# A hybrid decoder on one core: a second set of slots for the experts' down weights, an unrolled pair of rounds, and norms by token halves

## The reference

```python
def swiglu(h, w_gate, w_up, w_down):
    return (jax.nn.silu(h @ w_gate) * (h @ w_up)) @ w_down

def moe_swiglu(h, router_w, w_gate, w_up, w_down):
    ...
    for e in range(N_EXPERTS):
        y = swiglu(tokens, w_gate[e], w_up[e], w_down[e])
        out = out + combine[:, e:e + 1].astype(tokens.dtype) * y
```

## Time and profile before

| | us |
|---|---|
| median of 3 runs (2118.75 to 2121.64) | 2120.52 |
| the profiled execution, its own time | 2123.79 |
| its span | 2122.0 |
| TensorE matmuls busy | 1998.0 (94%) |
| TensorE weight loads busy | 1767.4 (83%) |
| VectorE / ScalarE / GpSimd busy | 403.7 / 271.6 / 87.8 |

### The profile page before, as it was taken

The page is one execution under the profiler, slowest core; times in us unless marked ns, Lnnn a source line. Parts: engine busy times, 40 slices in busy tenths (PEclk is TensorE's granted clock), DMA queues, the critical chain, the costliest instruction groups (busy, mean ns, idle before and its releaser), DMA issues.

```text
span 2122.0 us, 66421 instructions
## 1 busy us (share of the span) xinstructions
PE 1998.0 (94%) x31038; PEld 1767.4 (83%) x31038; DVE 403.7 (19%) x896; ACT 271.6 (13%) x572; POOL 87.8 (4%) x174
## 2 busy tenths in 40 slices
PE   7999989998999899999899969999999999999997
PEld 6888867887777688888678869998989898989896
DVE  3235331111000142353311130101010100000001
ACT  1213213001000112132220010000000000000001
POOL 4010111000000001011000000000000000000000
PEclk9899999999999999999899989999999999999999
DMA  7313112436741332221134549999999999999996
GB/s 232 119 42 120 41 41 67 132 119 223 234 157 40 119 107 74 80 80 42 41 111 147 216 169 397 407 407 407 407 407 407 407 407 407 407 407 407 407 407 251
DMA packets 214758, 482.90 MB, mean 228 GB/s; under 512 B 11582, under 2 KB 110092, under 8 KB 214668
## 3 DMA queue, kind: packets, MB, share of 16 engines
q1 hardware_dynamic: 214668, 481.54, 60.9%
HBM read 480.46 MB, written 1.05 MB: 227 GB/s over the span
## 4 chain that ended last, share of the span: by engine, by line
PE 83%; DMA 6%; DVE 4%; SPq 4%; ACT 1%; issue 1%; POOL 0%; DVEq 0%
PE bank L1089 29%; PE bank L598 21%; PE bank L1058 7%; DMA pool<-in_moe_w_down_dram 6%; PE bank L660 5%; PE bank L1012 4%; PE bank L1040 4%; SPq L1996 3%; PE bank L1027 3%; PE bank L1198 1%; PE bank L623 1%; SPq L2001 1%; PE bank L652 1%; PE bank L976 0%; DVE pool L1713 0%
## 5 line engine op out<-in xcount | busy, mean ns | idle before, releaser
L1089 PE MATMUL bank<-pool 128*64 128x80 f32 x21504 | 757.1, 234 | 32.8 <-DMA pool<-in_moe_w_down_dram 26.4
L1089 PEld LDWEIGHTS bank<-pool 128*64 128x64 f32 x21504 | 752.4, 138 | 38.8 <-issue 28.8
L598 PE MATMUL bank<-hnT,pool 128*128 128x256 f32 x1984 | 464.1, 389 | 1.6 <-DVE hnT L1537 1.6
L598 PEld LDWEIGHTS bank<-hnT,pool 128*128 128x128 f32 x1984 | 376.9, 194 | 62.6 <-issue 8.1
L1058 PEld LDWEIGHTS bank<-hnT,pool 128*128 128x128 f32 x704 | 133.7, 190 | 27.8 <-issue 9.6
L1058 PE MATMUL bank<-hnT,pool 128*128 128x256 f32 x704 | 155.5, 379 | 0.8 <-DVE hnT L1537 0.8
L1907 DVE TENSOR_TENSOR pool<-pool,bank 128x320 f32<-128x320 f32 x32 | 15.6, 488 | 639.1 <-ACT pool L1492 639.1
L660 PEld LDWEIGHTS bank<-pool 64*64 64x64 f32 x3008 | 96.0, 135 | 18.1 <-issue 11.5
L660 PE MATMUL bank<-pool 64*64 64x64 f32 (+1 forms) x3008 | 105.2, 221 | 5.6 <-DVE pool L1563 4.6
L1492 ACT ACTIVATE pool<-bank 128x320 f32<-128x320 f32 x32 | 14.0, 437 | 677.2 <-PE bank L1089 677.2
L547 POOL TENSOR_TENSOR pool<-pool,level_mask 128x256 f32<-128x256 f32 x72 | 52.0, 735 | 838.8 <-DVE pool L1639 538.4
(11 more groups left out here) (324 smaller groups left out, 1284.0 us busy)
## 6 DMA issues: line engine op xcount, KB each, us to landing
pool<-in_moe_w_up_dram SPq DMA_DIRECT2D x128, 896.0 KB, 16.6
pool<-in_moe_w_gate_dram SPq DMA_DIRECT2D x128, 896.0 KB, 16.5
pool<-in_w_in_dram SPq DMA_DIRECT2D x66, 1024.0 KB, 5.4
pool<-in_moe_w_down_dram SPq DMA_DIRECT2D x64, 1024.0 KB, 16.7
pool<-in_moe_w_down_dram SPq DMA_DIRECT2D x32, 1536.0 KB, 18.6
pool<-in_ffn_w_gate_dram SPq DMA_DIRECT2D x11, 1024.0 KB, 11.3
pool<-in_ffn_w_up_dram SPq DMA_DIRECT2D x11, 1024.0 KB, 7.8
pool<-in_ffn_w_down_dram SPq DMA_DIRECT2D x11, 1024.0 KB, 9.7
```

The lines of the kernel that those rows point to most:

```text
L598: ins = mm(ps[:, s * T:(s + 1) * T], w[:, k, (j + s) * P:(j + s + 1) * P], hnT[:, k, :], start=(k == 0), stop=(k == KD - 1))
L1089: ins = mm(bank[rows, cs], w[:, rows], rhs, start=start, stop=stop, skip_group_check=True)
```

## The change

- **Down weights in two sets.** `down_slot(n, p)` has a set for even and one for odd rounds. The second set's first load (round 1 of the first pass) is asked for after the last output projection; in the loop the down weights of round r + 2 are asked for when round r is done with its set. The places are where the merge's tensors lay.
- **PE's loops.** The loop over rounds runs NR // 2 = 2 times over a body of two rounds (p = 0 and 1). The loop over passes runs one time less, and the last pass is a second copy of the body, without the next pass's gather and selection rows. DVE's program is split the same way. SP's loop over rounds is written out.
- **Norms by token halves.** The output projection runs token tile by token tile; squares, Ln, Exp, scaling and transposes are issued per tile, those of tile 0 before the last quarter of the projection; the table load comes first. So too behind the dense part, where a signal is given after tile 0's last down matmuls.
- **RWKV order.** Its tiles are projected in the order (6, 2, 3, 0, 1, 4, 5). The LoRA matmuls come after 2 steps instead of all 26 that are left, then 8 own steps, kk2, the other 16, and 4 attention steps in place of 5 + 2 + 6; each of the two solver runs takes 3 instead of 2.
- **End.** x times the gain goes to its own place (xf) beside the squares; the factor is then applied to tile 0 by ACT and to tile 1 by DVE.

```diff
-        def down_slot(n):
-            lo = 2 * KH * HSLOT
+        def down_slot(n, p):
+            lo = 2 * KH * HSLOT + p * FB * D
             return pool[:, lo + 2 * n * D:lo + min(2 * n + (3 if n == 2 else 2), FB) * D].rearrange("p (f n) -> p f n", n=D)
...
-                all_of(projections)
-                some(steps, 5)
+                some(projections, 2)
                 lora_in.wait(pe, l, 1)
                 oa_ready.wait(pe, l, 2)
                 if l == 0:
...
-                some(steps, 2)
+                some(projections, 8)
                 kk2_ready.wait(pe, l, 1)
                 for q in range(2):
                     kk2_mm.by(mm(B[4 + q][:, :], same_chunk[:], rsq[:, 2 * q:2 * q + 2, :], start=True, stop=True))
-                some(steps, 6)
+                all_of(projections)
+                some(steps, 4)
...
-                    solver(l, 1 + q, steps, (2, 4))
+                    solver(l, 1 + q, steps, (2, 3, 4))
...
-                for half in range(2):
-                    for t in range(NT):
-                        if half == 0 and t == 0:
-                            merge_step.wait(pe, l, 12)
-                            oc_ready.wait(pe, l, 4)
-                        bank = B[2 * half + t]
+                merge_step.wait(pe, l, 12)
+                oc_ready.wait(pe, l, 4)
+                for t in range(NT):
+                    for half in range(2):
+                        bank = B[2 * t + half]
                         for s in range(2):
                             n = L[l]["out"][2 * half + s]
-                            arrived(n)
+                            if t == 0:
+                                arrived(n)
                             for k in range(KD):
                                 ins = mm(bank[:, s * SW:(s + 1) * SW], mT[:, k, t * P:(t + 1) * P], weights(n)[:, k, :],
                                          start=(k == 0), stop=(k == KD - 1))
                         xo_mm.by(ins)
-                    for s in range(2):
-                        release(L[l]["out"][2 * half + s], xo_mm)
+                        if t == 1:
+                            for s in range(2):
+                                release(L[l]["out"][2 * half + s], xo_mm)
+                        if t == 1 and half == 0:
+                            transposes_of_hn(l, 1, 0)
+                xo_ready.wait(pe, l, 2)
+                transposes_of_hn(l, 1, 1)
...
+                        if t == 0 and f == FFD // P - 1:
+                            down_mm.by(ins)
                     if i == loads[n][1][0] - 1:
                         down_mm.by(ins)
...
-                with pe.Fori(0, n_pass) as i:
+                def one_pass(i, last):
                     pe.wait_ge(xg_ready, i * 2 + 2)
                     pe.wait_ge(selT_ready, i + 1)
                     for half in range(2):
                         mm(B[4 + half][:, 0:4 * CAP], zeros[:, 0:P], zeros[:, :], start=True, stop=False,
                            skip_group_check=True)
-                    with pe.Fori(0, NR) as j:
+                    with pe.Fori(0, NR // 2) as j:
...
-                        hidden()
-                        down(0)
-                        down(1)
-                    pe.wait_ge(sc_added, i * 4 + 4)
-                    gather(i + 1)
+                        for p in range(2):
+                            hidden(p)
+                            down(p, 0)
+                            down(p, 1)
+                    if not last:
+                        pe.wait_ge(sc_added, i * 4 + 4)
+                        gather(i + 1)
...
-                    pe.wait_ge(xg_ready, i * 2 + 4)
+                    if not last:
+                        pe.wait_ge(xg_ready, i * 2 + 4)
...
-                    pe.wait_ge(sc_added, i * 4 + 5)
-                    selection_rows(i + 1)
+                    if not last:
+                        pe.wait_ge(sc_added, i * 4 + 5)
+                        selection_rows(i + 1)
+                with pe.Fori(0, more) as i:
+                    one_pass(i, False)
+                one_pass(more, True)
...
-                if half == 1:
-                    xo_ready.wait(act, l, 4)
-                elif l:
-                    fx_ready.wait(act, 0, 1)
-                for t in range(NT):
-                    if l == 0 and half == 0:
+                if half or l:
+                    ln_exp_tables()
+                for t in range(NT):
+                    if half:
+                        xo_ready.wait(act, l, 2 * t + 2)
+                    elif l:
+                        fx_ready.wait(act, 0, t + 1)
+                    else:
                         act.wait_ge(x_loaded[t], 16)
                     ins = A(hn[:, t, :], x[:, t, :], ACT.Square, accum_out=stat[:, 32 + t:33 + t])
-                ln_exp_tables()
-                link(ins)
-                link(A(stat[:, 34:36], stat[:, 32:34], ACT.Ln, scale=1.0 / D, bias=eps_c[:, 0:1]))
-                rms_ready.by(A(stat[:, 36:38], stat[:, 34:36], ACT.Exp, scale=-0.5))
+                    if t == 0 and l == 0 and half == 0:
+                        ln_exp_tables()
+                    link(ins)
+                    link(A(stat[:, 34 + t:35 + t], stat[:, 32 + t:33 + t], ACT.Ln, scale=1.0 / D, bias=eps_c[:, 0:1]))
+                    rms_ready.by(A(stat[:, 36 + t:37 + t], stat[:, 34 + t:35 + t], ACT.Exp, scale=-0.5))
...
-                all_of(raws)
-                raw_used.wait(act, l, 13)
+                next(raws)
+                raw_used.wait(act, l, 7)
...
-            act.wait_ge(all_added, 1)
             for t in range(NT):
+                act.wait_ge(all_added, t + 1)
                 ins = A(hn[:, t, :], x[:, t, :], ACT.Square, accum_out=stat[:, 32 + t:33 + t])
             link(ins)
             link(A(stat[:, 34:36], stat[:, 32:34], ACT.Ln, scale=1.0 / D, bias=eps_c[:, 0:1]))
             A(stat[:, 36:38], stat[:, 34:36], ACT.Exp, scale=-0.5).then_inc(frms_ready, 1)
+            act.wait_ge(frms_ready, 1)
+            act.wait_ge(xf_ready, 2)
+            A(xf[:, 0, :], xf[:, 0, :], ACT.Copy, scale=stat[:, 36:37]).then_inc(fin0_ready, 1)
...
+                residual(0, 0)
+                residual(0, 1)
+                scaled(l, 1, 0)
+                residual(1, 0)
+                turned(l, 1, 0)
+                residual(1, 1)
+                scaled(l, 1, 1)
+                turned(l, 1, 1)
...
-            v.memset(rs[:, 60:61], 0.0).then_inc(all_added, 1)
-            v.wait_ge(frms_ready, 1)
             v.wait_ge(fgain_loaded, 16)
             for t in range(NT):
-                stt(x[:, t, :], x[:, t, :], stat[:, 36 + t:37 + t], fgain, ALU.mult, ALU.mult).then_inc(fin_ready, 1)
+                v.wait_ge(all_added, t + 1)
+                ins = tt(xf[:, t, :], x[:, t, :], fgain, ALU.mult)
+            ins.then_inc(xf_ready, 1)
+            v.wait_ge(xf_ready, 2)
+            v.wait_ge(frms_ready, 1)
+            ts(xf[:, 1, :], xf[:, 1, :], stat[:, 37:38], None, ALU.mult).then_inc(fin_ready, 1)
...
+            xo_mm.wait(sp_, DEPTH - 1, 4)
+            for n in range(3):
+                lo, size = down_rows(n)
+                down_load(n, 1, slice(0, 1), slice(FB * P + lo, FB * P + lo + size))
...
-            def later_round(e, col, hid, dwn):
+            def hidden_round(i, r, e):
 
                 for n in range(2 * KH):
-                    sp_.wait_ge(hid_used, hid + (n + 1))
-                    hidden_load(n, bass.ds(e, 1), bass.ds(col, FB * P))
+                    sp_.wait_ge(hid_used, i * (2 * KH * NR) + (2 * KH * r + n + 1))
+                    col = (r + 1) % NR * FB * P
+                    hidden_load(n, e, slice(col, col + FB * P))
+            def down_round(i, r, e):
                 for n in range(3):
                     if n < 2:
-                        sp_.wait_ge(dwn_used, dwn + 1)
+                        sp_.wait_ge(dwn_used, i * NR + (r + 1))
                     else:
-                        sp_.wait_ge(dwn_mm, dwn * 2 + (down_base + 2))
+                        sp_.wait_ge(dwn_mm, i * (2 * NR) + (2 * r + down_base + 2))
                     lo, size = down_rows(n)
-                    down_load(n, bass.ds(e, 1), bass.ds(col + lo, size))
-            def rest_of_pass(i, e):
-                with sp_.Fori(0, NR - 1) as j:
-                    later_round(e, j * (FB * P) + FB * P, i * (2 * KH * NR) + j * (2 * KH), i * NR + j)
+                    lo += (r + 2) % NR * FB * P
+                    down_load(n, r % 2, e, slice(lo, lo + size))
 
             more = sp_.value_load(pass_expert[0:1, MAX_PASSES + 1:MAX_PASSES + 2], min_val=MIN_PASSES - 1,
                                   max_val=MAX_PASSES - 1)
             with sp_.Fori(0, more) as i:
                 e = sp_.value_load(pass_expert[0:1, bass.ds(i + 1, 1)], min_val=0, max_val=NE - 1)
-                rest_of_pass(i, e)
+                e = bass.ds(e, 1)
+                for r in range(NR - 2):
```

(23 more changed lines are left out.)

153 lines of the change are left out of this document (83 added, 70 removed).

## The result

| | before | changed |
|---|---|---|
| median time | 2121.08 us (2118.75 to 2122.73, 4 runs) | 2336.97 us (2333.86 to 2340.21, 4 runs) |
| ratio, 95% interval | | 1.1019 (1.0998 to 1.1040) |
| profiled execution: time, span | 2123.79, 2122.0 us | 2340.21, 2338.5 us |
| mean granted clock | 0.974 | 0.957 |
| first expert matmul | 1254.04 us | 1242.51 us |

The change costs 216 us, 10%. The direction and the mechanism were forecast, but 2337 lies over the range of 2105 to 2300: the size was missed.

A forecast was written before the change was run, and what follows sets the result against it. The DMA was taken to bound the experts, with 5.2 us of TensorE slack a pass. 2123.8 + 132 - 2.6 - 5.5 - 5 - 4 = 2238.7 for the profiled execution; median 2235 us, range 2105 to 2300.

The forecast's parts named there:

- What bounds: Experts' passes: they run at the DMA's rate, 108.2 us a pass, with only 5.2 us of slack on TensorE.
- Part 2: TensorE's expert loops: the two-round body, some 2,710 instructions, makes passes 124 us; +132 us in total.
- fetched again: TensorE's expert loops: each block of 256 instructions comes again by DMA each time, instead of being kept.
- No row shows a loop so long: TensorE's expert loops: no profile row shows loops of 10.6 and 11.3 blocks; the nearest kept was 7 blocks.
- I take the middle of 109 and 140, 124 us a pass: Experts' pass time with instructions fetched again: 124 us, chosen between 109 and 140.
- the rival of the full queue: Experts: every fetch meets a full queue, 140 to 150 us a pass, up to 2360 us; chance 0.06.
- Part 1: Experts' second set of down slots: early first load gains 9.0 us if DMA stays the bound, nothing if TensorE does.
- Parts 3 to 5: Ahead of the experts: norms behind output projection -2.6 (layer 1), norm behind dense part -5.5, RWKV order -5 us.
- Layer 0's turn of the gain into a DMA wait: Layer 0's norm behind the output projection: the gain becomes a wait for dense weights, so 0 us.
- Part 6: The end, behind the last down matmul: -2.3 without the gather and -1.6 from the final norm, -4 us.
- The loop is kept: TensorE's expert loops: new blocks cost only at first sight; 2117 us, between 2108 and 2125; chance 0.22.
- The fetches hide: Experts: later fetches are hidden, DMA stays the bound and all parts count; 2094.5 us; chance 0.06.

The follow-up runs named there:

- the silent run: Both kernels without the expert loads behind the first ones, so DMA is idle in the experts: 2077.11 us (kernel before), 2115.03 us (changed kernel), one run each.

## Why the prediction missed

**What bounds.** Right: the experts ran at the DMA's rate with little slack on TensorE. The slack is a bit more than I had, 6.3 us (108.2 less 101.9).

**Part 2, the mechanism.** Right in kind: "fetched again", 24 to 26 packets a pass, 267 in all, idle time on "issue", the DMA under 400 GB/s, longer waits at the branches back. "No row shows a loop so long" is settled by the runs with added matmuls.

**Part 2, the size.** The step that failed is "I take the middle of 109 and 140, 124 us a pass"; it measured 137.5. By pieces: to TensorE's 103 that step adds 21 us of waiting. The measured waiting is 25.0, so this was nearly right, between the ends of 5 and 47 that were worked out (the 1.5 us to start a fetch, in the lower end, named no row; with the DMA idle the whole fetch behind the inner branch takes 2.9 to 3.3 us, where 2.6 was taken). What the term left out is **the clock**. I had it only in the rival of the full queue, "some 2 us each time, 15 times", and it came in the forecast's own case: 10.6 us more of busy time in a pass at a granted clock of 0.93, some 8 of it in stretches under 1.00. The 326 records behind the two branches take 13.72 and 13.21 us; at the silent run's 93.19/2,688 = 34.7 ns they would take 11.3. That is 4.3 us, and two stretches behind gaps of 2.0 and 2.3 us have 3.9 more. Per pass the miss is 13.5 us (4.0 of waiting and 10.6 of busy time, less 1.1 by which TensorE's own pass is under 103), seven times 94.5; the last pass took 118.9 instead of 115. Together 98 of the 101.5 us by which the sum (2238.7) fell short of the profiled execution (2340.2).

The reason given for going under 140, that "a DMA that waits for TensorE has short queues" and a fetch waits less there, held only by half. The queues are shorter, loads land in 7.5 to 9.0 us (medians) where they took 16.5 to 18.6, but a block still comes up to 2.3 us late. The windows show why: the DMA doesn't run at four fifths all the time, it runs at 411 GB/s and is idle in turns. It is idle behind the branches (0.51 and 186 GB/s), and full while TensorE crosses blocks, since it is TensorE's progress that releases loads.

**Part 1, second set: -9 if the DMA bounds, nothing if TensorE does.** The second case came, so nothing was the right term: a pass takes 137.2 us without the set and 137.5 with it. The run with the set on a DMA-bound kernel shows no gain there either, but with new code beside it, so the 9.0 is neither shown nor refuted.

**Parts 3 to 5, ahead of the experts: -13.1, measured -11.5 in one pair of profiles.** The dense end was right: the last dense matmuls end at 733.19 and the next projection starts at 739.85, 6.7 us where it was 12.0, so 5.4 for the forecast 5.5; tile 0's adds start at 731.52, 1.7 us ahead of that end, as the forecast has it. Layer 0's turn of the gain into a DMA wait was right, with 9.1 us instead of 10.0, but the clock was left out here too: behind a wait of 4.6 us the first 64 records of the dense part take 16.88 us at a granted clock of 0.83, where they took 14.08 at 1.00. Layer 1's norm: from the end of the projection to the first matmuls behind the router's (L1079, now L1092) 17.8 us before (1223.06 to 1240.84) and 15.4 now (1213.56 to 1228.92), so 2.4 for 2.6; tile 0's transposes, moved ahead, cost 0.9 there. RWKV's order was right in kind (one wait gone, a new one of 2.4 us) and too small: in layer 1, from the first projection behind the dense part to the output projection, 449.6 us became 444.9 in this pair, so -4.7 for -2.5. In layer 0 the pair shows 2.2 us (493.58 for 495.80), but that is within what executions of the same code differ by at this place.

**Part 6, the end: -4, measured -2.6.** From the last down matmul to the end of the execution 18.6 us before (2105.2 to 2123.8), now 16.0 (2324.2 to 2340.2). By the run without the experts' edits (16.7 us to the span's end, 16.8 before) the final norm's -1.6 brought 0.1; what was gained is the gather's share, as the run with the copy alone shows (13.7).

**Rivals.** "The loop is kept" had 0.22. Its deciding point was put at twelve blocks; the runs put it at eight. "The fetches hide" (0.06) is what the silent run shows, but not with weights on the DMA. "Every fetch meets a full queue" (0.06) was nearest in time and right about the clock; it should have had more, with its clock term taken into the forecast.

## What to carry to other kernels

Count the instructions of a loop on TensorE before unrolling it, from the head of the outermost loop that must be kept to its end, in blocks of 256, and keep one block free for the one asked for ahead: over eight, the whole loop comes again by DMA, here at up to 2.3 us a block and some 6 us behind the inner branch while weights stream, and then the clock falls behind the longer waits. Price a new wait on a busy TensorE with what it does to the clock afterwards. Code that is run once is cheap where its engine would wait for data anyway: the last pass's copy cost 5.6 us of gaps and saved 3.4 of waits.

## What was not expected of the hardware

- The limit is sharp and not in proportion: 64 one-number matmuls in the pass cost nothing that one run shows (2123.43), 128 cost 81 us (2202.57 against the 2121 of before), though they run for some 3.4 us a pass. At the edge (96) the same loop was kept in five turns and lost in two.
- The wait behind the inner branch is 2.9 to 3.3 us with idle DMA engines and 5.0 to 6.3 with weights on them, in seven passes each; with a hint ahead of the branch it was 5.9 to 7.1, and the time 2349.57 us instead of 2336.97.
- Behind waits of 3 to 6 us TensorE's granted clock was 0.81 to 0.89 in the 13 to 14 us of matmuls that followed, with weights streaming or (0.83 over 10 us) without. Behind waits of about 2 us it fell at times (0.89 over 15.4 us, 0.74 over 6.2) and at times not: a wait of 1.96 us ahead of 1547.54 left the next stretch at 1.00. The window of such a stretch in the run with 128 added matmuls:

```profile
1367.15:1381.28 14.13, 14.13 (x330) 13.97 (x327) 0.00 (x0) 0.00 (x0) 0.00 (x0) 0.81 0.49 180
```
